# Combining one group's expert rows on chip while the other rows are read back, in a two-layer mixture-of-experts step

## The chip, the cores and the metric

One NeuronCore of a Trainium2 chip runs the whole program. The metric is the device time of one execution in microseconds (us). Three timed runs of the kernel before gave 1610.86, 1612.04 and 1613.86 us; a further execution was profiled.

## What is computed

A transformer trunk of two layers on 384 tokens of width 1024 (128 of a context pass, 256 of a denoising pass): layer 0 mixes tokens by differential attention, layer 1 by retention. Each mixer is followed by a mixture of experts, 16 experts in 4 groups of 4. All in float32.

```python
def group_moe(h, w_router, router_bias, w_gate, w_up, w_down):
    t = h.reshape(B * N, D)                       # D = 1024, 384 tokens in all
    s = sigmoid(t @ w_router)
    sel = s + router_bias
    grp_score = top_k(sel.reshape(-1, 4, 4), 2)[0].sum(-1)
    best = argmax(grp_score)                      # one group for each token
    _, idx = top_k(where(in_group, sel, -inf), 2) # two experts of that group
    gates = one_hot(idx) * normalised(s at idx)
    for each expert e:                            # w_gate, w_up: 1024 x 512, w_down: 512 x 1024
        y += (silu(t @ w_gate[e]) * (t @ w_up[e]) * gates[e]) @ w_down[e]
```

The layer then adds a per-feature gate times y to x, and a normalisation follows.

## The kernel before

**Engines.** Each engine runs its own list of instructions in order, and semaphores tie the lists together. PE (TensorE) multiplies, DVE (VectorE) and ACT (ScalarE) move and combine results, POOL (GpSimd) does some elementwise work and the indirect reads, SP issues the weight loads. `x` is kept transposed on chip as `xT`, features on partitions.

**Weights.** A ring of six slots of 2 MB holds weight units: three for each expert (gate, up, down), in the order of use. SP refills a slot when its last user is done: expert e's gate and up slots when the gate and up matmuls of expert e-2 and its overflow are done, the down slot when its down matmuls are (L530 issues).

**Routing** (`experts(l)` on DVE, L1455 to L1548). The logits and the normalisation come out of PE; DVE picks the group and the two experts of each token in some 40 small chained operations, PE computes each token's rank in its expert (L814, L816), and DVE makes the one-hot selection `sel` of pairs of experts (L1519). Meanwhile PE turns the scaled x into token rows `htok` (L807, six pieces of 128x512); ACT scales them (L1177) and POOL adds the shift (L1705).

**Experts** (PE, L880 to L915). Experts go two by two through x = 0, 1. Up to 64 tokens of an expert are gathered by one-hot matmuls from `htok` (L828) into `xs`. For expert e: gate and up (L892, L893: each 64 columns of the array), silu on ACT (L1210), the product on DVE (L1592), four transposes (L904), part of the next pair's gather, down (L913, L914), a copy by DVE (L1596), and a store of the 64 rows to the HBM table `expert_rows` by ACT (L1218). A further loop handles overflow in blocks of 32 tokens for an expert with more than 64 (L850 to L873, its rows stored by L1198). The number of blocks is read from a table at run time.

**Read-back.** When all 16 experts' rows are stored, POOL reads two rows for each token by six indirect DMAs (`pick_rows`, L1755), DVE weighs and adds them into `ytok` (L1600, L1601), PE turns `ytok` (L921, 8 jobs of three transposes), and DVE adds each times the gate to `xT` (L1363). The squares for the next norm follow on ACT (L1062).

**Order.** `plan_jobs` lists every use of a PSUM bank in PE's order, with the engine that empties it; jobs take the eight banks in turn. `plan_units` lists the weight units.

## Time and profile before

| | us |
|---|---|
| median of three runs | 1612.04 |
| profiled execution | 1609.19 |
| its span (first to last instruction) | 1607.4 |
| PE busy | 1390.9 |
| VectorE busy | 416.1 |
| ScalarE busy | 260.6 |
| GpSimd busy | 74.7 |
| data moved by DMA | 345.75 MB, mean 215 GB/s |

The span is what the trace covers; 1.8 us of the profiled execution lie around it. Busy PE means that matmuls are in flight. Layer 0's experts lie at about 386 to 703 us, layer 1's at 1233 to the end. L-numbers are lines of the kernel before.

### The profile page before, as it was taken

To read this page: it belongs to the slowest core of one execution; us is meant where nothing else is said; L and a number is where in the kernel's file an instruction comes from. 1 tells how busy PE (TensorE), PEld (TensorE's weight loads), DVE (VectorE), ACT (ScalarE), POOL (GpSimd) and SP (SyncE) were. 2 spreads that over 40 slices of the span, in tenths; PEclk is the share of its full clock that TensorE was granted. 3 is DMA by queue.
4 is the path that set the end of the run, shared out by engine and by line. 5 is a ranking of instruction groups with operands and counts; after the bars stand their busy time and mean duration, and the time that the engine had idled before them with its cause. 6 is when DMAs were issued, how large, how long until landed. Compare 5 with 4: busy or idle time off the path is not lost.

```text
span 1607.4 us, 16614 instructions
## 1 busy us (share of the span) xinstructions
PE 1390.9 (87%) x6404; PEld 729.0 (45%) x6404; DVE 416.1 (26%) x1138; ACT 260.6 (16%) x546; POOL 74.7 (5%) x97
## 2 busy tenths in 40 slices
PE   5997998698998988479999999998797898988863
PEld 3544655365443434144454544544454543443422
DVE  3234515524111111051250521603203211011113
ACT  3133114212110100021110221202102101010002
POOL 2110000001000000100000000000002000000001
PEclk9998998798999999879999999999799899999986
DMA  9888329514999998653233332333022499999403
GB/s 343 318 261 294 113 69 363 209 53 158 379 396 398 395 397 333 216 183 105 105 105 105 105 105 92 118 104 126 29 81 105 182 396 397 396 395 366 173 21 118
DMA packets 162734, 345.75 MB, mean 215 GB/s; under 512 B 5193, under 2 KB 22770, under 8 KB 162626
## 3 DMA queue, kind: packets, MB, share of 16 engines
q1 hardware_dynamic: 149906, 319.24, 54.1%
q10 hardware_dynamic: 9776, 15.34, 2.7%
q0 software_dynamic: 2944, 9.65, 2.1%
q8 instruction: 77, 1.26, 0.3%
q14 instruction: 31, 0.25, 0.0%
HBM read 324.95 MB, written 19.27 MB: 214 GB/s over the span
## 4 chain that ended last, share of the span: by engine, by line
PE 73%; DMA 11%; issue 6%; DVE 5%; ACT 3%; SPq 1%; POOL 0%; DVEq 0%; ACTq 0%; POOLq 0%
PE psum L699 18%; PE psum L892 11%; PE psum L692 10%; DMA ring<-in_moe_w_up 9%; PE psum L1007 5%; PE psum L913 5%; PE psum L828 4%; PE psum L796 3%; PE psum L992 3%; PE psum L594 2%; PE psum L861 2%; DMA ring<-in_w_ada 1%; PE psum L601 1%; PE psum L873 1%; PE psum L757 1%
## 5 line engine op out<-in xcount | busy, mean ns | idle before, releaser
L699 PE MATMUL psum<-ring,hT 128*128 128x512 f32 x672 | 289.4, 592 | 0.0
L892 PE MATMUL psum<-ring,work 128*64 128x512 f32 x512 | 234.9, 613 | 24.6 <-DMA ring<-in_moe_w_up 15.6
L893 PE MATMUL psum<-ring,work 128*64 128x512 f32 x512 | 235.3, 614 | 0.0
L699 PEld LDWEIGHTS psum<-ring,hT 128*128 128x128 f32 x672 | 127.5, 190 | 158.9 <-issue 157.8
L692 PE MATMUL psum<-hT,ring 128*128 128x384 f32 x512 | 170.9, 493 | 3.3 <-DVE hT L1348 3.3
L892 PEld LDWEIGHTS psum<-ring,work 128*64 128x64 f32 x512 | 71.2, 141 | 173.2 <-issue 172.8
L913 PE MATMUL psum<-ring,work 128*64 128x512 f32 x256 | 122.5, 623 | 11.4 <-issue 11.3
L692 PEld LDWEIGHTS psum<-hT,ring 128*128 128x128 f32 x512 | 98.6, 193 | 71.7 <-issue 6.0
L914 PE MATMUL psum<-ring,work 128*64 128x512 f32 x256 | 122.7, 624 | 0.0
L828 PE MATMUL psum<-work 128*128 128x128 f32 x768 | 107.1, 292 | 13.2 <-issue 10.9
L828 PEld LDWEIGHTS psum<-work 128*128 128x128 f32 x768 | 95.5, 200 | 37.4 <-issue 32.8
L1592 DVE TENSOR_TENSOR work<-work,psum 64x512 f32<-64x512 f32 x32 | 22.1, 690 | 242.3 <-ACT work L1210 242.3
L1596 DVE COPY work<-psum 128x512 f32<-128x512 f32 x32 | 22.1, 692 | 203.4 <-PE psum L914 203.4
L1210 ACT ACTIVATE work<-psum 64x512 f32<-64x512 f32 x32 | 18.8, 588 | 339.4 <-PE psum L893 339.4
L893 PEld LDWEIGHTS psum<-ring,work 128*64 128x64 f32 x512 | 71.1, 141 | 0.0
L913 PEld LDWEIGHTS psum<-ring,work 128*64 128x64 f32 x256 | 33.9, 143 | 73.5 <-issue 70.6
L1363 DVE SCALAR_TENSOR_TENSOR xT<-psum,mod,xT 128x128 f32<-128x128 f32 x64 | 22.5, 411 | 124.9 <-PE psum L1007 83.4
L796 PE MATMUL psum<-sq,ring 128*128 128x384 f32 x128 | 44.2, 507 | 9.0 <-DVE sq L1444 9.0
L921 PE MATMUL psum<-base_sb,sq 128*128 128x128 f32 x48 | 9.6, 390 | 46.8 <-issue 46.8
L594 PE MATMUL psum<-ring,cond 128*32 128x512 f32 x384 | 44.5, 603 | 3.7 <-DMA ring<-in_w_ada 3.7
L1007 PE MATMUL psum<-sq,ring 128*128 128x384 f32 x128 | 45.1, 507 | 0.9 <-ACT hT L1228 0.9
L1641 DVE TENSOR_SCALAR work<-psum,work 128x256 f32<-128x256 f32 x4 | 1.9, 485 | 167.1 <-PE psum L958 167.1
(287 smaller groups left out, 1394.1 us busy)
## 6 DMA issues: line engine op xcount, KB each, us to landing
ring<-in_moe_w_gate SPq DMA_DIRECT2D x32, 2048.0 KB, 17.2
ring<-in_moe_w_up SPq DMA_DIRECT2D x32, 2048.0 KB, 22.1
ring<-in_moe_w_down SPq DMA_DIRECT2D x32, 2048.0 KB, 19.2
ring<-in_w_ada SPq DMA_DIRECT2D x24, 2048.0 KB, 12.2
ring<-in_da_w_qkv SPq DMA_DIRECT2D x6, 2048.0 KB, 17.1
expert_rows<-work ACTq DMA_DIRECT2D x64, 128.0 KB, 5.6
ring<-in_ret_w_qkv SPq DMA_DIRECT2D x8, 1024.0 KB, 7.9
ring<-in_ret_w_qkv SPq DMA_DIRECT2D x4, 2048.0 KB, 8.0
```

The costliest lines, as they stand in the source:

```text
L594: last = mm(b[32 * j:32 * j + 32, :], cond[:, kt, :], w[:, kt, :], start=kt < 4, stop=kt >= 4)
L692: last = mm(b[:, 0:TOK], w[:, kt, col:col + P], hT[:, kt, :], start=kt == 0, stop=kt == KT - 1)
L699: last = mm(b, hT[:, kt, P * t:P * t + P], w[:, kt, :], start=kt == 0, stop=kt == KT - 1)
L796: last = mm(b[:, 0:TOK], w[:, h, P * (ft % 4):P * (ft % 4) + P], oT[:, h, :], start=h == 0, stop=h == HEADS - 1)
L828: last = mm(out, htok[:, t, P * kt:P * kt + P], sel[:, t].rearrange("p x s -> p (x s)"), start=t == 0, stop=t == TT - 1)
L861: last = mm(ov[OVB * j:OVB * j + OVB, 0:QC], ox[:, kt, :], w[:, kt, QC * (j % 2):QC * (j % 2) + QC], start=kt == 0, stop=kt == KT - 1)
L892: mm(psum[0:BLK, x, :], xk, wg[:, kt, :], start=kt == 0, stop=kt == KT - 1)
L893: last = mm(psum[BLK:P, x, :], xk, wu[:, kt, :], start=kt == 0, stop=kt == KT - 1)
L913: mm(psum[0:BLK, 5 + x, :], eaT[:, x, k, :], wd[:, k, 0:512], start=k == 0, stop=k == 3)
L914: last = mm(psum[BLK:P, 5 + x, :], eaT[:, x, k, :], wd[:, k, 512:D], start=k == 0, stop=k == 3)
L992: last = mm(b, a, v, start=n == 0, stop=n == len(terms) - 1)
L1007: last = mm(b[:, 0:TOK], w[:, k, P * (ft % 2):P * (ft % 2) + P], roT(k), start=k == 0, stop=k == 15)
```

## The change

The groups go in the order 3, 2, 1, 0 (router columns and bias are loaded in this order). The last group's rows (experts 12 to 15 in the new order, `LAST` = 12) are no longer stored: for each of these experts DVE makes a one-hot matrix times the gates (`selw`), PE turns it (`wT`), and matmuls of the expert's rows with `wT` give a contribution to y in feature layout, which DVE adds to `xT`. This is done while the next expert's gate and up run, two feature blocks behind every second k step; expert 15's come after its down. The rows of the first 12 experts are read back by POOL after expert 11; ACT and DVE weigh them at expert 13, and PE turns `ytok` in experts 14 and 15. Tokens of the last group read row 0 with weight zero. Gate and up of expert 2 go to two spare places outside the ring (`spare`), loaded before the experts start. The ring slots of gate and up are free when the expert's activation is transposed (`T`), not when gate and up are done. The token rows are scaled and shifted by one DVE operation, and POOL's additions go.

```diff
+GROUPS = (3, 2, 1, 0)
+LAST = NE - EPG
+def side_plan():
+    pair = lambda e, i: [("comb", e, i, 4), ("comb", e, i + 4, 7)]
+    turn = lambda i: [("turn", None, i, 2), ("turn", None, i + 1, 3)]
+    plan = {(e, 2 * i + 1): pair(e - 1, i) for e in range(LAST + 1, NE) for i in range(4)}
+    plan[(NE - 2, "T")] = turn(0)
+    for i in range(3):
+        plan[(NE - 1, 2 * i)] = turn(2 * i + 2)
...
-        out = [(("htok", layer, i), "act") for i in range(2 * TT)]
+        out = [(("htok", layer, i), "dve") for i in range(2 * TT)]
...
+        spare = [(sq, wm["yg"][:, 2 * D:3 * D]), (hT, wm["yg"][:, 0:D])]
...
+    def moe_unit(r):
+        return divmod(r if r < 6 else r + 2, 3)
...
-                for q in range(1, NE // 2):
-                    for x in range(2):
-                        e = q * 2 + x
-                        ov = sp.value_load(RT[l][0:1, e - 1:e], min_val=0, max_val=OVMAX)
-                        sp.wait_ge(m["gu"], e - 1)
-                        settle(sp, l)
-                        sp.wait_ge(m["o_down"], ov + 1)
-                        settle(sp, l)
-                        expert_load(x, 0, e)
-                        expert_load(x, 1, e)
-                        sp.wait_ge(m["down"], e - 1)
-                        settle(sp, l)
-                        expert_load(x, 2, e)
+                filled(sp, ("rwo" if l else "wo", KT - 1))
+                spare_load(0)
+                filled(sp, ("htok", l, 2 * TT - 1))
+                for i in range(2 * TT):
+                    emptied(sp, ("htok", l, i))
+                spare_load(1)
+                for r in range(6, 3 * NE - 2):
+                    e, part = moe_unit(r - 6)
+                    sp.wait_ge(m["down" if part == 2 else "T"], e + 1)
+                    settle(sp, l)
+                    expert_load(r)
...
+                def combine(e, kt, out):
+                    rows = slice(BLK * (kt // 4), BLK * (kt // 4) + BLK)
+                    return mm(out, ysb[rows, e % 2, P * (kt % 4):P * (kt % 4) + P], wT[rows, :], start=True, stop=True)
+                def side_work(at):
+                    for kind, e, kt, place, n, before_, _ in side.get(at, ()):
+                        if before_:
+                            pe.wait_ge(m["side_added"], before_)
+                        if kind == "comb":
+                            pe.wait_ge(m["y"], e + 3)
+                            pe.wait_ge(m["wT"], e - LAST + 1)
+                            last = combine(e, kt, psum[:, place, 0:TOK])
+                        else:
+                            pe.wait_ge(m["xs"], NE)
+                            pe.wait_ge(m["ytok"], TT)
+                            for t in range(TT):
+                                last = tr(psum[:, place, P * t:P * t + P], ytok[:, t, P * kt:P * kt + P], ident)
+                        last.then_inc(m["side"], 1)
...
                             last.then_inc(m["T"], 1)
+                            if e >= LAST:
+                                pe.wait_ge(m["selw"], e - LAST + 1)
...
+                                for t in range(TT):
+                                    last = tr(psum[:, 4, P * t:P * t + P], selw[:, t].rearrange("p n s -> p (n s)"), ident)
+                                last.then_inc(m["selT"], 1)
+                            side_work((e, "T"))
...
-                pe.wait_ge(m["ytok"], TT)
+                pe.wait_ge(m["y"], NE + 2)
+                pe.wait_ge(m["wT"], EPG)
+                pe.wait_ge(m["side_added"], side_count)
                 for ft in range(KT):
                     b = open_job(("y", l, ft))
-                    for t in range(TT):
-                        last = tr(b[:, P * t:P * t + P], ytok[:, t, P * ft:P * ft + P], ident)
-                    done(last)
+                    done(combine(NE - 1, ft, b[:, 0:TOK]))
...
+                            if e >= LAST:
+                                act.wait_ge(m["selT"], e - LAST + 1)
+                                A(wT, psum[:, 4, 0:TOK], ACT.Copy).then_inc(m["wT"], 1)
...
+                            if e == LAST + 1:
+                                act.wait_ge(m["picked"], 32 * TT)
+                                for t in range(TT):
+                                    A(ytok[:, t, :], yg[0][:, t, :], ACT.Copy, scale=wt_all[:, 0, t:t + 1]).then_inc(m["half"], 1)
...
+                def token_rows(half):
+                    for t in range(TT):
+                        i = TT * half + t
+                        filled(dve, ("htok", l, i))
+                        V.scalar_tensor_tensor(out=htok[:, t, 512 * half:512 * half + 512], in0=bank(("htok", l, i)), scalar=rin[:, t:t + 1],
+                                               in1=shrow[:, min(t, 1), half, :], op0=ALU.mult, op1=ALU.add).then_inc(evac["dve"], 1)
...
+                token_rows(0)
                 b3 = rbias[:, :].unsqueeze(1).broadcast_to([P, TT, NE])
...
                 dve.wait_ge(m["chosen"], 1)
...
+                token_rows(1)
...
+                def side_work(at):
+                    for kind, e, kt, place, n, _, added in side.get(at, ()):
+                        if added:
+                            dve.wait_ge(m["side_added"], added)
+                        dve.wait_ge(m["side"], n + 1)
+                        add_rows(psum[:, place, :], kt).then_inc(m["side_added"], 1)
...
+                            if e >= LAST:
+                                weigh_slots(e)
+                            for kt in range(KT):
+                                side_work((e, kt))
...
+                            if e == LAST + 1:
+                                for t in range(TT):
+                                    dve.wait_ge(m["half"], t + 1)
+                                    V.scalar_tensor_tensor(out=ytok[:, t, :], in0=yg[1][:, t, :], scalar=wt[:, 1, t:t + 1], in1=ytok[:, t, :],
+                                                           op0=ALU.mult, op1=ALU.add).then_inc(m["ytok"], 1)
...
+            for g in range(NG):
+                here, there = slice(EPG * g, EPG * g + EPG), slice(EPG * GROUPS[g], EPG * GROUPS[g] + EPG)
+                pool.dma_start(rbias[:, here], ins["router_bias"].unsqueeze(0)[:, there].broadcast_to([P, EPG])).then_inc(in_bc, 16)
+                pool.dma_start(wr[:, :, here], ins["w_router"].rearrange("(k p) e -> p k e", p=P)[:, :, there]).then_inc(in_bc, 16)
...
-                pool.wait_ge(m["stored0"], 32 * (NE // 2 + 1))
+                pool.wait_ge(m["stored0"], 32 * (LAST // 2 + 1))
...
-            add_shift(1)
+            pool.wait_ge(M[1]["routed"], 1)
             for kt in range(KT):
                 G.tensor_scalar(gdiag[:, kt, :], ident, cols1[:, kt:kt + 1], None, ALU.mult).then_inc(gdiag_ready, 1)
```

Overflow blocks of the last group (experts 12 to 15) would be combined in the same way; those of the others are stored as before.

## Rows read from the trace of the kernel before

**Rows 1.** The page's chain of work that ended last, by line.
```profile
PE psum L699 18%; PE psum L892 11%; PE psum L692 10%; DMA ring<-in_moe_w_up 9%; PE psum L1007 5%; PE psum L913 5%; PE psum L828 4%; PE psum L796 3%; PE psum L992 3%; PE psum L594 2%; PE psum L861 2%; DMA ring<-in_w_ada 1%; PE psum L601 1%; PE psum L873 1%; PE psum L757 1%
```

**Rows 2.** Windows: stretch, its length, busy time by engine, granted clock, DMA share, GB/s.
```profile
410.00:600.00 190.00, 173.95 (x908) 81.63 (x906) 21.91 (x42) 18.83 (x36) 0.00 (x0) 0.96 1.04 397
...
666.00:690.00 24.00, 0.61 (x5) 0.53 (x4) 6.63 (x7) 0.00 (x0) 5.78 (x6) 0.61 0.66 219
1563.00:1587.00 24.00, 0.61 (x4) 0.39 (x3) 6.63 (x7) 0.00 (x0) 5.74 (x6) 0.56 0.44 142
```

**Rows 3.** Timeline (start, length, both us) behind layer 0's last expert, all engines.
```profile
666.15 0.69 DVE L1596 COPY work<-psum 128x512 f32<-128x512 f32 x1 [4.79 <-PE psum L914]
666.87 1.13 ACTq L1218 DMA_DIRECT2D expert_rows<-work  x2
670.87 1.05 POOL L1755 DMA_INDIRECT work<-expert_rows,work  x1 [291.05 <-issue]
...
677.23 0.94 POOL L1755 DMA_INDIRECT hT<-expert_rows,work  x1 [0.30 <-issue]
...
683.36 0.75 DVE L1600 TENSOR_SCALAR sq<-work 128x1024 f32<-128x1024 f32 x1 [16.52 <-DMA hT<-expert_rows,work]
...
689.50 0.87 PE L921 MATMUL psum<-base_sb,sq 128*128 128x128 f32 x3 [23.39 <-issue]
```

**Rows 4.** Timeline behind layer 1's last expert, PE's restart.
```profile
1586.64 0.66 PE L921 MATMUL psum<-base_sb,sq 128*128 128x128 f32 x2 [23.39 <-issue]
```

**Rows 5.** Timeline of PE: first gate matmuls of experts 0, 2, 3, 6, 12, 13, 14; 0, 13, 14.
```profile
394.17 0.64 PE L892 MATMUL psum<-ring,work 128*64 128x512 f32 x1
...
423.10 0.59 PE L892 MATMUL psum<-ring,work 128*64 128x512 f32 x1
...
437.01 0.59 PE L892 MATMUL psum<-ring,work 128*64 128x512 f32 x1
...
484.35 0.61 PE L892 MATMUL psum<-ring,work 128*64 128x512 f32 x1 [1.37 <-issue]
...
586.60 0.59 PE L892 MATMUL psum<-ring,work 128*64 128x512 f32 x1
...
601.60 0.61 PE L892 MATMUL psum<-ring,work 128*64 128x512 f32 x1 [0.92 <-DMA ring<-in_moe_w_up]
...
626.80 0.59 PE L892 MATMUL psum<-ring,work 128*64 128x512 f32 x1
...
1258.09 0.64 PE L892 MATMUL psum<-ring,work 128*64 128x512 f32 x1
...
1475.46 0.59 PE L892 MATMUL psum<-ring,work 128*64 128x512 f32 x1
...
1511.30 0.59 PE L892 MATMUL psum<-ring,work 128*64 128x512 f32 x1
```

**Rows 6.** The page's DMA issues: count, KB each, median us to landing.
```profile
ring<-in_moe_w_up SPq DMA_DIRECT2D x32, 2048.0 KB, 22.1
```

**Rows 7.** Timeline of PE in layer 0, of VectorE in layer 1.
```profile
369.72 2.82 PE L807 MATMUL psum<-base_sb,hT 128*128 128x128 f32 x24
...
1228.73 0.74 DVE L1363 SCALAR_TENSOR_TENSOR xT<-psum,mod,xT 128x128 f32<-128x128 f32 x2 [8.99 <-PE psum L1007]
```

**Rows 8.** Timeline of GpSimd and VectorE, at the start and in layer 0's routing.
```profile
44.06 0.72 POOL L1735 TENSOR_TENSOR work<-work 128x256 f32<-128x256 f32 x1 [6.55 <-ACT work L1100]
...
372.38 7.43 POOL L1705 TENSOR_TENSOR work<-work 128x512 f32<-128x512 f32 x6 [154.65 <-ACT work L1177]
...
373.73 1.21 DVE L1485 TENSOR_TENSOR work<-work,base_sb 128x12 f32<-128x12 f32 x1
...
380.40 0.21 DVE L1485 TENSOR_TENSOR work<-work,base_sb 128x48 f32<-128x48 f32 x1
```

**Rows 9.** The chain of work in order of time: start, us, what.
```profile
182.63 5.16 PE psum L692 x16
```

**Rows 10.** Groups of instructions: busy us, mean ns, idle before.
```profile
L1554 DVE SCALAR_TENSOR_TENSOR work<-work,base_sb 128x96 f32<-128x96 f32 x39 | 10.0, 256 | 1.3 <-issue 0.4
```

More of the change, by code:

```diff
@@ L179, in plan_units @@
     units += [(("ada", l, u), ("ada", l, u)) for l, u in NORM_UNITS]
-    units += [(("moe", 0, n), None) for n in range(3 * NE)]
+    units += [(("moe", 0, n), None) for n in range(3 * NE - 2)]
     for h in range(RH):
@@ L184, in plan_units @@
     units += [(("rwo", n), ("rwo", 2 * n + 1)) for n in range(4)]
-    units += [(("moe", 1, n), None) for n in range(3 * NE)]
+    units += [(("moe", 1, n), None) for n in range(3 * NE - 2)]
     return units
@@ L820, in experts @@
                 u0 = unit_no[("moe", l, 0)]
-                emptied(pe, ("rank", l))
+                for i in range(2 * TT):
+                    emptied(pe, ("htok", l, i))
                 def gather(half, kts):
@@ L1759, in _ @@
             pool.sem_inc(M[1]["o_down"], 1)
-            add_shift(0)
             pick_rows(0)
```

259 lines of the change are left out of this document (171 added, 88 removed).

## The prediction

> **What bounds the kernel now.** I read the chain that ended last, by line, first: TensorE's matmuls hold most of it, and one transfer stands out, the experts' up weights with 9% [rows 1]. Then the stages: through 190 us of the first layer's experts the DMA engines move 397 GB/s at a busy share of 1.04 while PE is busy 174 us; in the 24 us after the last expert of either layer PE works 0.6 us and the transfers run at 219 and 142 GB/s [rows 2]. So there are two bounds: weight traffic while experts run, and a latency chain behind them. The timeline shows that chain: the last copy of expert rows at 666.15, the store issued at 666.87, six indirect reads from 670.87 to 678.2 whose last lands at 683.3 (what VectorE's wait ends on), six weighting operations, and PE's transposes at 689.50 after 23.39 us of idleness; layer 1 has the same 23.39 [rows 3, 4]. Last, the starts of the experts on PE. Undisturbed an expert takes 437.01 - 423.10 = 13.9 us. Where weights bound it, six take 586.60 - 484.35 = 102.3, so 17.0 each, with some restarts of PE in it. One expert moves 3 x 2.097 MB plus 0.26 MB of stored rows, 6.55 MB, at 397 GB/s 16.5 us [rows 2, 5, 6]; I use 16.7. An expert with one overflow block takes 626.80 - 601.60 = 25.2, one with two 1511.30 - 1475.46 = 35.8 [rows 5]: 11.3 and 22 more. The trace has two blocks in layer 0 (experts 13, 14) and five in layer 1 (12 to 15, expert 13 twice): all in the group that now comes first.
>
> **The sum's base.** The profiled execution took 1609.2 us (span 1607.4 and 1.8 around it), 2.8 below the median 1612.0. I sum against 1609.2 and add 2.8 at the end.
>
> **Head of the experts.** The token rows' scaling leaves ScalarE, the shift leaves GpSimd, both become one VectorE operation per piece. No row has it; a 128x128 and a 128x256 one with a PSUM input take 0.74 us together [rows 7], so 0.7 to 0.8 for 512 columns. Six cost 4.4 us in VectorE's chain, of which the last three replace a wait for the rank matmuls (about 2 us), so 1.5 + 0.7 are on the path. Removed is what GpSimd did to that chain: an operation on 12 columns takes 1.21 us while GpSimd's 7.43 us run, and on 48 columns 0.21 after it [rows 8]. Six operations are stretched so, to 0.8 to 1.2 each, about 5.4 us together. Net 3.1 us earlier in layer 0, 4.2 in layer 1 (four NORM additions fewer on the path, and GpSimd's eight diagonal products leave it too). Bounds 0 to 5 each. The moved diagonal products now run beside VectorE's index computation, 5 to 10 us long, which has the 8 us of the first gather and 7 us of the first gate and up as cover. The "GPSIMD Engine Reference" of the Trainium skill (its table's row on SBUF interfaces) says that GpSimd's SBUF interfaces are shared with VectorE. By it the index chain stretches as these rows did; the cover still holds it. The six more small loads on GpSimd's queue near the start, at 0.94 to 1.05 each as its other DMAs [rows 3], stay under the 6.55 us in which it idles there [rows 8]: nothing, else under 1 us.
>
> **Early overflow and the two spare weight slots.** Experts start at 391.1 instead of 394.17 [rows 5]. Expert 0 takes 13.9, experts 1 and 2 take 25.2, then 13.9 each: expert 4 starts at 469.3, expert 7 could at 511. A slot is now refilled after the activation's transpose, 9.6 us after an expert's start (7.0 gate and up, 2.3 gather, 0.4), so behind an overflow. The DMA queue runs dry three times while experts 1 and 2 are long, about 25 us in all; the two spare slots let PE not feel it. It is full from expert 3's transpose (465.0): the first load lands 9 us later (5.3 to move; the rest is an estimate from the reads' 6.1 between issue and landing [rows 3]) and each next one 5.57 (16.7 / 3), so expert 6's up weights land at 496.6, expert 7's at 513.3: from here the weights bound, 16.7 each. Expert 12 starts at 596.9 and 13 could at 613.6. In layer 1 the start is 1253.9, expert 0 takes 25.2, 1 takes 36, 2 and 3 take 25.2, expert 7 starts at 1409.1, 12 at 1492.6. The DMA queue is never dry after that: at a transpose some four units are queued ahead.
>
> **The read-back moves into this stretch.** Expert 11 ends at 594. Between its last store and the first read lay 4.0 us in a half idle queue [rows 3]; I take twice that in a full one. Six indirect reads from 602.5, 1.25 to 1.3 apart as in the tail, are issued by 610 [rows 3]. Their 3.1 MB take 7.9 us of the DMA engines at 397 GB/s. Expert 13's weights are late by all of it or, where reads share the queue with loads already due, by 5: it starts at 618.6 to 621.5. That gives 5 to 8 us per layer of the tail back. What weighs the rows has slack: PE needs them after expert 14's transposes, at about 652, ScalarE's wait for them is reached at about 634, and they are there by about 622. The "DMA: Bandwidth & Descriptors" page of the Trainium skill (Queues, rings and completion order) says that a DMA engine takes its queues in turn, packet by packet. By it the reads get half the engines beside the full load queue, 16 us, and land at 622 as said; no row shows two full queues.
>
> **Added work in the last group.** A combining matmul has 64 partitions and 384 columns; the nearest rows, 16 records for 8 matmuls of 384 columns in 5.16 us, give 0.645 each [rows 9]; below, half of that, if two run at a time. Eight per expert for 13, 14 and 15: 5.2 us (2.6 to 5.2; I take 5.2). Turning the weighted one-hot rows: three transposes, 24 take 2.82 us at full clock [rows 7], so 0.35. The turns of ytok, 24, 2.8, moved off the tail. On VectorE each of these feeds an add of 0.74 (0.82 if the two halves don't overlap) [rows 7], plus seven small operations per expert near the 0.26 us row [rows 10], 1.8.
> Expert 12: 14.3. Expert 13: 13.9 + 5.2 + 0.35, 19.6. Expert 14, bound by VectorE: copy 0.75, the three ytok operations 3.9 (three pairs took 6.14, the other half 0.75 each [rows 3]), 1.8, eight adds 6.6, gating 0.7, then transposes, down and its waits 5.5: 19.3. Expert 15: 7.0 + 5.2 + 2.1 on PE against 14.1 on VectorE, then gating and the rest, 19.8. Nothing hides these except the weights' own pace: expert 14's are there at 637, so it is PE and VectorE that bound the last three.
> Last down in layer 0: 618.6 or 621.5 + 19.6 + 19.3 + 19.8 = 677.3 to 680.2. Layer 1: 1572.6 to 1575.5.
>
> **The tail.** Store, reads, weighting and 23.39 us of idleness go; what is left is the copy (0.69) and a semaphore, 0.9. PE restarts at 678.2 to 681.1 instead of 689.50, and at 1573.5 to 1576.4 instead of 1586.64 [rows 3, 4]: 8.4 to 11.3 and 10.2 to 13.1 gained. The eight last combinations, 5.2 us, replace 24 transposes that took 5.4 after the idleness. I take 10 and 11.5. The granted clock was 0.61 and 0.56 in the idle stretches [rows 2] and should stay higher now, worth 1 to 2 us after each; I set that against as much lost where PE changes between halves and whole arrays. The "TensorEngine Tiling (Array Packing)" page of the Trainium skill (Key Properties) says that a change of tiling mode drains TensorE, which speaks against this change: 24 changes per layer. By it a few us more would be lost; no row of mine separates it.
> 1609.2 - 10 - 11.5 = 1587.7, plus 2.8: **1590.5 us**.
>
> **Rivals.**
> (a) *The pairs of combinations run side by side* on the two halves of the array, and the reads cost only what they overlap: expert 13 falls by 2.6, expert 15's PE part drops below VectorE's, the reads cost 5. 4 to 5 per layer: 1582. For it: an expert's 24 matmuls of 512 columns at the price of rows 9 would be 20.6 us, more than its whole 13.9 [rows 5], so pairs on column halves do overlap. Against: VectorE still bounds 14 and 15. The same skill page (Tiling Modes) has two 64x128 tiles, and would give this.
> (b) *The read-back is not hidden*: stores, six reads and the full load queue take over 30 us instead of 22, ScalarE sits in its wait with expert 14's activation behind it, and PE behind that. For it: full engines from 596 on. Against: 12 us of slack. Some 5 to 8 us late per layer: 1604.
> (c) *Slower: VectorE's adds bound the last two experts.* Each add waits for its matmul, its predecessor and a bank, and PE waits for the add before it reuses bank 4 or 7. With 22 adds in experts 14 and 15, 10.8 us per layer are gone when an add costs 0.5 us more than 0.8: from 1.3 us on the change is slower. At 1.7 it is 1590.5 + 2 x 22 x 0.9 = 1630; at 1.5, 1621. For it: every add is in lockstep with PE. Against: 0.74 measured, and in the old tail eight came 0.66 apart.
> (d) *The change only moves the time*: the dry queue costs more than I find, because PE catches up with the weights already at expert 5, and with 8 us of reads the end of the experts moves 10 us more per layer: 1610.
>
> **Chances.** Forecast 0.62, (a) 0.14, (b) 0.10, (c) 0.07, (d) 0.07. Its own range is 1585 to 1598. The range that takes in (a) and most of (b), and the bounds of head and combinations, is 1576 to 1606. A difference under 0.2%, 3 us, can't be told from none. Faster: the forecast, (a), (b) and a little of (d), 0.87; same 0.05; slower 0.08.
>
> **What would show it.** Right: PE idle under 1.5 us after the last down; gather about 3 to 4 us earlier; small VectorE operations there at 0.2; DMA below 300 GB/s while experts 0 to 3 run and 397 after 4; expert 13 with the longest wait for weights; last three experts 19 to 20 each. Wrong: ScalarE waiting for the reads (b), adds above 1.3 us apart (c), the weights' wait beginning at expert 5 (d), combinations 0.32 apart (a). The whole is wrong if the last expert ends later than 689 or 1586.

## The result and the profile after

The changed kernel took 1617.4 us (median of 20 runs, 1607.5 to 1620.2), the kernel before 1610.3 (20 runs, 1602.8 to 1616.8): a ratio of 1.0031, 95% interval 1.0017 to 1.0046. I had forecast 1590.5 with a range that ended at 1606. The change costs about 5 us by this ratio (7 by the medians) where I expected 21 to be gained.

The profiled execution of the changed kernel took 1607.5 us (span 1605.6), the shortest of its twenty, so its total may not be laid beside the 1609.2 of before. Its stages may. From the first turn of the token rows to the first product of the next stage, layer 0 took 707.05 - 362.28 = 344.8 us against 702.94 - 369.72 = 333.2 before: 11.6 longer. Layer 1, to the end, took 1605.65 - 1236.45 = 369.2 against 373.8: 4.6 shorter. Together 7.0 slower, near what the medians say. What this execution has less lies elsewhere: 7.4 us ahead of layer 0's experts, in code that the change hardly touches, and 1.2 between the two layers. The output product of the first mixer started at 308.12; in a second profile of the same kernel at 319.92, in the one before at 315.59, and in all fifteen profiles of this study between 308 and 321. In the second profile the two stages of experts, each as a whole, have the same length to 0.3 us.

Head and tail went as forecast. PE's rows of the head, layer 0 and layer 1 (the token rows' first turn, the gather, expert 0):
```profile
362.28 0.52 PE L844 MATMUL psum<-base_sb,hT 128*128 128x128 f32 x3
...
374.55 8.54 PE L866 MATMUL psum<-work 128*128 128x128 f32 x48 [2.44 <-DVE work L1634]
...
383.02 0.64 PE L980 MATMUL psum<-ring,work 128*64 128x512 f32 x1
...
1236.45 0.41 PE L844 MATMUL psum<-base_sb,work 128*128 128x128 f32 x2
...
1255.07 0.64 PE L980 MATMUL psum<-ring,work 128*64 128x512 f32 x1
```
Expert 0 starts 20.7 and 18.6 us after the first turn, where it was 24.45 and 24.55: 3.7 and 5.9 gained (forecast 3.1 and 4.2). VectorE's operation on 48 columns at the gather takes 0.20 and none of the small ones is stretched to the 1.2 us of [rows 8].

The tail of both layers, all engines:
```profile
692.79 0.69 DVE L1769 COPY work<-psum 128x512 f32<-128x512 f32 x1 [6.48 <-PE psum L1012]
...
693.54 4.24 PE L947 MATMUL psum<-work 64*128 64x384 f32 x16 [0.79 <-DVE work L1769]
...
694.55 5.29 DVE L1468 SCALAR_TENSOR_TENSOR xT<-psum,mod,xT 128x128 f32<-128x128 f32 x16 [1.07 <-PE psum L947]
...
1584.90 4.24 PE L947 MATMUL psum<-work 64*128 64x384 f32 x16 [0.79 <-DVE work L1769]
```
PE restarts 0.75 us after the copy begins; it was 23.35 [rows 3, 4]. From the last down product to the next stage 14.3 and 21.6 us are left of 36.9 and 44.1.

So the loss is among the experts: from expert 0 to the last down product 309.7 us instead of 271.9 in layer 0, 329.0 instead of 305.1 in layer 1. Windows (columns as in [rows 2]): experts 4 to 11, then experts 13 to 15 of layer 0 and of layer 1.
```profile
466.00:595.00 129.00, 116.46 (x612) 54.48 (x608) 15.40 (x29) 12.55 (x24) 0.00 (x0) 0.97 1.04 396
```
```profile
618.92:692.72 73.80, 62.50 (x261) 24.01 (x261) 32.83 (x86) 8.09 (x13) 0.00 (x0) 0.86 0.67 245
1516.18:1584.08 67.90, 60.05 (x261) 21.87 (x261) 32.74 (x86) 8.09 (x13) 0.00 (x0) 0.89 0.56 214
```
The three experts that I had put at 58.7 us take 73.8 and 67.9. VectorE is busy 33 us of them and the DMA engines 0.67 and 0.56 of the time. PE is busy 60 to 62.5 us, at a mean granted clock of 0.86 to 0.89 (0.97 in the experts before). So nothing but PE is near full, and PE is often at its lower clock level. That is how it would look if PE and VectorE waited for each other; the experiments test it. PE's first gate products of experts 12, 13, 14 and 15:
```profile
595.20 0.61 PE L980 MATMUL psum<-ring,work 128*64 128x512 f32 x1 [0.65 <-issue]
...
618.92 1.09 PE L980 MATMUL psum<-ring,work 128*64 128x512 f32 x1 [8.12 <-DMA ring<-in_moe_w_up]
...
645.61 0.59 PE L980 MATMUL psum<-ring,work 128*64 128x512 f32 x1
...
670.36 0.59 PE L980 MATMUL psum<-ring,work 128*64 128x512 f32 x1
```
Expert 13 waits 8.12 us for its weights, then takes 26.7; expert 14 takes 24.8, expert 15 22.4. Layer 1 has 21.0, 26.2 and 20.7. I had put 19.6, 19.3 and 19.8, so the excess is 7.1, 5.4 and 2.6 in layer 0 and 1.4, 6.9 and 0.9 in layer 1.

The 7.1 of expert 13 in layer 0 are mostly something else. Between the first and the second of the transposes of its activation PE stands still, and the profile shows nothing that it waits for ("issue"):
```profile
638.22 0.48 PE L994 MATMUL psum<-base_sb,work 64*128 64x64 f32 x3 [3.35 <-issue]
```
From these transposes to the down product it takes 6.15 us instead of 1.54 in layer 1, and the down product, partly at the lower clock level, 5.03 instead of 3.65: 6.0 us together. The trace has a DMA queue that it calls "instruction", with loads of 16 KB. One starts at 635.68, inside the stop, and PE goes on 2.54 us later. Ten profiles of the changed kernel and its variants have a stop at this very transpose, of 0.6 to 3.4 us, and in all ten PE goes on 2.3 to 2.6 us after such a load's start. So PE probably waits there for instructions; no run varies this alone.

Expert 14 of layer 1 shows how the waits arise (all engines, from the copy of expert 13's rows to the transposes):
```profile
1537.39 0.69 DVE L1769 COPY work<-psum 128x512 f32<-128x512 f32 x1 [5.92 <-PE psum L1012]
...
1538.11 3.68 DVE L1773 SCALAR_TENSOR_TENSOR sq<-hT,work,sq 128x1024 f32<-128x1024 f32 x3
...
1538.99 0.92 PE L947 MATMUL psum<-work 64*128 64x384 f32 x4
...
1541.71 0.25 DVE L1679 SCALAR_TENSOR_TENSOR work<-work,base_sb 128x96 f32<-128x96 f32 x1
1541.88 0.85 DVE L1684 TENSOR_SCALAR work<-base_sb,work 128x128 f32<-128x128 f32 x3
1542.65 0.85 DVE L1690 TENSOR_SCALAR work<-base_sb,work 128x128 f32<-128x128 f32 x3
1543.41 1.39 DVE L1696 SCALAR_TENSOR_TENSOR xT<-psum,mod,xT 128x128 f32<-128x128 f32 x4
...
1544.21 2.29 PE L947 MATMUL psum<-work 64*128 64x384 f32 x4 [2.44 <-DVE xT L1696]
...
1546.43 1.11 PE L980 MATMUL psum<-ring,work 128*64 128x512 f32 x1
...
1554.48 1.39 DVE L1696 SCALAR_TENSOR_TENSOR xT<-psum,mod,xT 128x128 f32<-128x128 f32 x4 [1.32 <-PE psum L947]
1555.90 0.69 DVE L1763 TENSOR_TENSOR work<-work,psum 64x512 f32<-64x512 f32 x1
...
1556.74 0.43 PE L994 MATMUL psum<-base_sb,work 64*128 64x64 f32 x4 [2.36 <-DVE work L1763]
```
PE's first pair of combinations of expert 13's rows (four records, two products) runs at 1538.99 and takes 0.92 us. Its adds could follow at once, but VectorE is in ytok's 3.68 us and then in the next slots' 1.95; they begin 3.5 us after the pair's end. PE stands 2.44 us before the next pair, and when it goes on its products of 512 columns take 1.11 us instead of 0.59: it has fallen to the 1.2 GHz level. At the end the gating stands behind the last two adds, and the transposes wait 2.36 us.

### The profile page after: what moved, and what is told of

The parts are those of the page before. It is cut to its first block, busy times and chain, and to the rows that moved or that the text cites. A ratio compares the mean times of both kernels' runs of the same rounds, so it can differ in the third digit from the quotient of the medians.

```text
span 1605.6 us, 17122 instructions
## 1 busy us (share of the span) xinstructions
PE 1425.1 (89%) x6556; PEld 731.6 (46%) x6556; DVE 466.5 (29%) x1332; ACT 263.9 (16%) x548; POOL 64.3 (4%) x91
## 4 chain that ended last, share of the span: by engine, by line
PE 75%; DMA 11%; DVE 6%; ACT 3%; issue 3%; SPq 1%; DVEq 0%; POOL 0%; ACTq 0%; POOLq 0%
PE psum L736 18%; PE psum L980 11%; PE psum L729 10%; DMA ring<-in_moe_w_up 9%; PE psum L1104 5%; PE psum L866 5%; PE psum L1011 5%; PE psum L833 3%; PE psum L1089 3%; PE psum L947 2%; PE psum L918 2%; PE psum L631 2%; DMA ring<-in_da_w_qkv 1%; PE psum L930 1%; PE psum L794 1%
## 5 line engine op out<-in xcount | busy, mean ns | idle before, releaser
L980 PE MATMUL psum<-ring,work 128*64 128x512 f32 x480 | 228.8, 623 | 33.0 <-DMA ring<-in_moe_w_up 21.8
L981 PE MATMUL psum<-ring,work 128*64 128x512 f32 x480 | 229.2, 624 | 0.0
L980 PEld LDWEIGHTS psum<-ring,work 128*64 128x64 f32 x480 | 64.9, 142 | 173.4 <-issue 173.2
L1011 PE MATMUL psum<-ring,work 128*64 128x512 f32 x256 | 121.9, 621 | 0.7 <-issue 0.5
L1012 PE MATMUL psum<-ring,work 128*64 128x512 f32 x256 | 122.0, 621 | 0.0
L981 PEld LDWEIGHTS psum<-ring,work 128*64 128x64 f32 x480 | 64.9, 142 | 0.0
L1011 PEld LDWEIGHTS psum<-ring,work 128*64 128x64 f32 x256 | 33.7, 142 | 63.2 <-issue 60.1
L1696 DVE SCALAR_TENSOR_TENSOR xT<-psum,mod,xT 128x128 f32<-128x128 f32 (+1 forms) x128 | 44.6, 410 | 50.2 <-PE psum L947 46.2
L1468 DVE SCALAR_TENSOR_TENSOR xT<-psum,mod,xT 128x128 f32<-128x128 f32 x64 | 22.5, 411 | 124.8 <-PE psum L1104 83.3
```

The costliest lines, as they stand in the source:

```text
L980: mm(psum[0:BLK, x, :], xk, wg[kt], start=kt == 0, stop=kt == KT - 1)
L981: last = mm(psum[BLK:P, x, :], xk, wu[kt], start=kt == 0, stop=kt == KT - 1)
L1011: mm(psum[0:BLK, 5 + x, :], eaT[:, x, k, :], wd[k][:, 0:512], start=k == 0, stop=k == 3)
L1012: last = mm(psum[BLK:P, 5 + x, :], eaT[:, x, k, :], wd[k][:, 512:D], start=k == 0, stop=k == 3)
L1696: last = V.scalar_tensor_tensor(out=xT[:, kt, a:z], in0=src[:, a:z], scalar=mod[:, l, 40 + kt, c:c + 1], in1=xT[:, kt, a:z], op0=ALU.mult, ...
```

## Experiments

All ratios are to the kernel before, which ran on the same chip beside each; "n us below the changed kernel" is the difference of two such ratios, with 1.0031 and 1.0015 for the changed kernel, times 1610; "last three" is from expert 13's first gate product to the last down product, layer 0 / layer 1, read from each run's trace.

**The same kernel again.**


> The changed kernel once more, unaltered. Its profiled execution so far took 1607.5 us, its median 1617.4, while the kernel before had 1609.2 and 1610.3. Theory 1 (the extra 10 us of a usual execution lie in the last group of four experts, where PE alternates with VectorE and falls to the lower clock level): this profile reads 1613 to 1619, the last three experts take 75 to 80 us in layer 0 and 69 to 75 in layer 1 (73.8 and 67.9 in the first profile), the attention part up to the output product stays near 308. Rival (the first profile only had a lucky attention part): the output product starts at 313 to 317 instead of 308.1, and the expert stages keep 309.7 and 329.0 within 2 us.


1615.3 us median of 12, ratio 1.0015 (0.9996 to 1.0034), the profiled execution 1619.2. Of the rival, the experts' half held: the stages agree to 0.3 us (309.6, 328.9; last three 74.1 / 68.0). The output product started late, at 319.92, even later than the 313 to 317 that it named.
```profile
319.92 1.65 PE L833 MATMUL psum<-sq,ring 128*128 128x384 f32 x2 [8.96 <-DVE sq L1549]
```
Theory 1 was wrong: the last three did not grow (it wanted 75 to 80 and 69 to 75), and the first mixer did. For all that follows I compare stages, not totals of single profiles.

**The order alone**, in the kernel before:
```
+GROUPS = (3, 2, 1, 0)
-w = (wg, wu, wd)[part][e].rearrange(...)
+w = (wg, wu, wd)[part][EPG * GROUPS[e // EPG] + e % EPG].rearrange(...)
```


> The kernel before with its groups in the order 3 to 0 and nothing else. Theory 1 (the order is neutral: the DMA queue is dry early instead of late): the stage from expert 0 to the last down product takes 268 to 276 us in layer 0 (271.9 before) and 298 to 306 in layer 1 (305.1), total within 5 us of the kernel before. Rival (the early overflow starves the queue and PE never gets it back): 280 or more in layer 0 and 313 or more in layer 1, total 1620 to 1630.


1610.1, ratio 0.9984 (0.9962 to 1.0005). Experts 272.1 and 306.1 us (271.9 and 305.1 before). Theory 1: overflow blocks cost the same at either end, so rival (d) of the prediction falls as far as it rests on the order. This trace shows one thing more: with the old ring of six slots expert 12 starts 206.6 and 239.3 us after expert 0, in layer 0 sooner than in any profile of the changed kernel (210.7 and 212.2), in layer 1 the same. Expert 0 took 14.6 us there in layer 0 and not 16.7 to 18.4. The two spare places and the later return of the slots bought nothing that these traces show.

**The head alone**, in the kernel before (token rows on VectorE, GpSimd's addition out, and as in the changed kernel seven small VectorE operations that normalise the routing weights moved behind the slot table, 1.5 us):
```
-A(htok[...], bank(("htok", l, i)), ACT.Copy, scale=rin[:, t:t + 1])
-G.tensor_tensor(cols, cols, shrow[:, min(t, 1), half, :], ALU.add)
+V.scalar_tensor_tensor(out=htok[...], in0=bank(("htok", l, i)), scalar=rin[...], in1=shrow[...], ...)
```


> The kernel before with the head's part alone: token rows scaled and shifted by VectorE in one operation, no GpSimd addition, the normalisation of the routing weights behind the slot table. Theory 1 (the head's gain is real and is kept by the weight-bound stage, because slots are refilled earlier too): expert 0 starts 3 to 4 us after the rows' first turn earlier than before in layer 0 (20.7 instead of 24.45) and 4 to 6 earlier in layer 1, total 1601 to 1605. Rival (weights bound the end of the stage anyway, the gain turns into a longer wait for weights): same starts, but the stages from expert 0 to the last down product are 3 to 5 us longer, total 1608 to 1612.


1598.8, ratio 0.9921 (0.9893 to 0.9950). Expert 0 starts 20.7 and 18.7 us after the first turn. In its one profile layer 0's experts took 276.0 us, 4.1 longer, of which experts 13 and 15 have 1.7 each, at granted clocks of 0.94 and 0.89 where it was 1.00, and layer 1's 305.5; the medians say that the gain is kept: 0.5 to 1.1%, 8 to 17 us. The head alone was worth more than half of what I had forecast for the whole change, and the rest of the change lost it all again and 5 us more.

**The changed kernel with the order 0 to 3.**
```
-GROUPS = (3, 2, 1, 0)
+GROUPS = (0, 1, 2, 3)
```


> The changed kernel with its groups in the order 0 to 3, so that the group with most overflow blocks is the one combined on chip. Theory 1 (order is neutral for the weights; the read-back of 3.1 MB, which delays expert 13 by 8 us when weights bound it, is hidden behind the overflow blocks of experts 13 and 14, but each block's own eight combinations and adds cost 6 us): expert 13 waits under 2 us for weights, two blocks in layer 0 and five in layer 1 add 12 and 30 us; total 1615 to 1635. Rival (order 3 to 0 is what loses, by the queue that is dry for 25 us): total 1600 or less.


1669.4, ratio 1.0366 (1.0335 to 1.0397). Worse than either theory. Experts 13 to 15, layer 0 and 1:
```profile
604.14:712.32 108.18, 82.92 (x547) 34.62 (x547) 49.79 (x138) 9.82 (x17) 0.00 (x0) 0.87 0.45 165
1496.71:1644.53 147.82, 105.46 (x835) 45.05 (x831) 69.34 (x198) 11.55 (x21) 0.00 (x0) 0.86 0.21 79
```
Expert 13, with one block in layer 0, took 43.1 us where it had taken 26.7 without one; expert 14 44.4 instead of 24.8. So a block whose rows are combined on chip costs 16 to 20 us, not 11.3. In layer 0 the read-back was not hidden either: expert 13 waited 6.7 us. In layer 1, behind the block of expert 12, it did not wait. The order is free in itself, but with on-chip combination it must be 3 to 0: for the data of this run that is worth 52 to 56 us.

**Without the side products.**
```
-plan = {(e, 2 * i + 1): pair(e - 1, i) for e in range(LAST + 1, NE) for i in range(4)}
+plan = {}
```


> The changed kernel without the 24 combining products of experts 12 to 14 and their adds on VectorE (this part of the sum is left out; the weighted rows, their turns, the read-back and expert 15's products stay). Theory 1 (the last group was mis-sized because the side products hold PE in lockstep with VectorE): from expert 13's start to the last down product 48 to 53 us in each layer instead of 73.8 to 76.1 and 68, the half clock stretches in expert 14 disappear, total 40 us below the changed kernel. Rival (ytok, the weighted rows and their turns are what holds it): 62 or more in either layer.


1583.7, ratio 0.9815 (0.9761 to 0.9868).
```profile
629.62:682.31 52.69, 45.88 (x213) 19.00 (x213) 16.21 (x38) 8.10 (x13) 0.00 (x0) 0.91 0.91 337
1511.18:1562.26 51.08, 44.94 (x213) 19.39 (x213) 16.12 (x38) 8.10 (x13) 0.00 (x0) 0.91 0.70 265
```
52.7 / 51.1, theory 1 in the stages, though the total is 32 to 35 us below the changed kernel and not 40: the 24 products and their adds cost 21 us in layer 0 and 17 in layer 1. Without them expert 13 of layer 0 has no stop at its transposes, so some 6 of the 21 may be that stop and the clock behind it. I had given the whole added work of the three experts 58.7 - 3 x 13.9 = 17 us, ytok and slots included.

**The products without VectorE's adds.**
```
-add_rows(psum[:, place, :], kt).then_inc(m["side_added"], 1)
+dve.sem_inc(m["side_added"], 1)
```


> The changed kernel with all its side products on TensorE but without VectorE's 32 adds of them per layer (the residual stream misses these rows); VectorE only passes the semaphore on. Theory 1 (VectorE's adds, not TensorE's products, are the price): the last three experts take 55 to 60 us, 10 to 18 less than in the changed kernel in each layer. Rival (the products and the changes between half and whole arrays cost as much by themselves): 65 or more.


1594.7, ratio 0.9879 (0.9824 to 0.9935).
```profile
627.88:690.23 62.35, 57.38 (x261) 22.00 (x261) 10.63 (x22) 8.09 (x13) 0.00 (x0) 0.91 0.79 290
1514.86:1571.50 56.64, 54.38 (x261) 20.55 (x261) 10.64 (x22) 8.09 (x13) 0.00 (x0) 0.96 0.67 254
```
62.4 / 56.6, a little over the forecast in layer 0. Taking out the adds saves 11.5 and 11.3 us. That is of all 32 adds, the eight behind the turns of ytok too, so the 24 have at most this share of the 21 and 17, and the products (with the stop in layer 0, which stays) at least the other 9.7 and 5.6. VectorE's busy time fell by 22 us, twice what the stretch lost: half of the adds' time had been hidden. Expert 14 without adds needs 10.0 us for gate and up with three pairs of products among them, 3.0 over the plain 7.0: 0.5 per product.

**Without the read-back.**
```
-pool.indirect_dma_start(out=yg[c][:, t, :], ...).then_inc(m["picked"], 16)   (six of them)
```


> The changed kernel without the six indirect reads (the rows of the first three groups are not read back). Theory 1 (they cost the weight stream exactly their own bytes): expert 13's wait for its weights shrinks from 8.1 to 9.3 us (7 to 8 in layer 1) to 1 to 3 us, as of the experts before it; the last three experts stay at 74 to 76 and 68; total 14 us below the changed kernel. Rival (the wait is that of the queue behind the early overflow): it stays above 5 us.


1598.1, ratio 0.9919 (0.9891 to 0.9947), theory 1. Expert 13's wait shrinks from 8.12 to 0.92 us (in layer 1 from 7.81 to 2.09):
```profile
617.73 0.61 PE L980 MATMUL psum<-ring,work 128*64 128x512 f32 x1 [0.92 <-DMA ring<-in_moe_w_up]
```
Expert 12 takes 16.5 us to the next start instead of 21.1 to 24.9; the last three 72.0 / 65.8, 2 us less: expert 13's first products now run at 0.61 us and its gate and up take 10.1 us instead of 12.1, PE no longer having stood still before them. So the read-back delays expert 13 by 4.6 to 8.4 us per layer, as forecast (5 to 8).

**ytok weighed earlier.** ScalarE's three scalings ahead of expert 13's activation, VectorE's three operations behind expert 13's gating:
```
-if e == LAST + 1: (after the copy of y)
+if e == LAST + 1: (after side_work((e, "T")), before dve.wait_ge(m["down"], e + 1))
     V.scalar_tensor_tensor(out=ytok[:, t, :], in0=yg[1][:, t, :], ...)
```


> The changed kernel with ScalarE's three scalings ahead of expert 13's activation and VectorE's three weighting operations behind expert 13's gating instead of ahead of expert 14's adds. Theory 1 (in expert 14 TensorE stands behind 3.7 us of weighting and 2 us of small operations in VectorE, loses about 5 us to it and 3 more to the lower clock level): expert 14's gate and up stretch falls from 14.8 to 16.4 us to 12 to 13, the three weighting operations vanish between expert 13's transposes and its down product, total 5 to 8 us below the changed kernel. Rival (VectorE is the bound of the whole stretch, so the 3.7 us only move into expert 13): under 2 us.


1605.0, ratio 0.9965 (0.9940 to 0.9989), 8 to 11 us below the changed kernel by the two ratios of that one; its experts' stages are 10.8 us shorter, more than expected. Last three 68.4 / 62.6. VectorE in layer 1, in expert 13 (the weighting) and 14 (two pairs of adds):
```profile
1529.39 3.68 DVE L1769 SCALAR_TENSOR_TENSOR sq<-hT,work,sq 128x1024 f32<-128x1024 f32 x3
...
1537.89 1.39 DVE L1696 SCALAR_TENSOR_TENSOR xT<-psum,mod,xT 128x128 f32<-128x128 f32 x4
1540.61 1.39 DVE L1696 SCALAR_TENSOR_TENSOR xT<-psum,mod,xT 128x128 f32<-128x128 f32 x4 [1.32 <-PE psum L947]
```
Gate and up take 10.0 us, as without any add: once VectorE arrives in time, its adds (1.39 of every 2.72 us) hide behind PE completely. 3.7 us of work in the wrong place cost 5.4 us of the last three in layer 0 and 5.3 in layer 1.

**Gating ahead of the last adds.**
```
-for kt in range(KT):
+for kt in range(KT - 1):
     side_work((e, kt))
 V.tensor_tensor(ea[...], sg[...], psum[...], ALU.mult).then_inc(m["gated"], 1)
+side_work((e, KT - 1))
```
and PE turns the weighted slots last before the down product.


> The changed kernel with VectorE's gating of experts 13 to 15 ahead of the last pair of adds instead of behind it, and the turn of the weighted one-hot rows issued last before the down product. Theory 1 (gating stands 1.4 us behind the two last adds, which nothing on TensorE needs that early): from the end of gate and up to the transposes 1.2 us less in each of the three experts (3.65 becomes 2.4 in expert 15), 3.5 per layer, total 6 to 8 us below the changed kernel. Rival (TensorE waits for the same adds anyway, before it reuses bank 4): under 2 us.


1608.6, ratio 0.9991 (0.9971 to 1.0011), 4 to 6 below the changed kernel, between the two theories; last three 68.3 / 64.0. The transposes' wait falls to 0.71 us (2.36 before), but the next turn then waits for the same adds:
```profile
1578.40 0.43 PE L994 MATMUL psum<-base_sb,work 64*128 64x64 f32 x4 [0.71 <-DVE work L1763]
...
1579.77 0.52 PE L1005 MATMUL psum<-base_sb,work 128*128 128x128 f32 x3 [0.94 <-DVE xT L1696]
```
Expert 15's down starts 0.8 us earlier, not 1.2; the larger part came from expert 14, 3.2 and 3.1 us shorter, where the down product also ran at the full clock (3.65 us, 4.2 and 5.35 before). A part of this gain is the clock's.

**Combinations in the wait for weights.**
```
+plan[(LAST + 1, -1)] = [job for i in range(4) for job in plan.pop((LAST + 1, 2 * i + 1))]
+side_work((e, -1))
 wg, wu = unit(e, 0), unit(e, 1)
```


> The changed kernel with expert 12's eight combinations ahead of expert 13's first weight instead of between its gate and up products. Theory 1 (TensorE stands idle there for 8 us, because the read-back takes them from the weight stream; the combinations with their adds, some 8 us in lockstep, fit into it): expert 13's gate and up stretch falls from 12.1 to 12.4 us to 7.0 to 8.8, its start moves by less than 1 us, total 7 to 9 us below the changed kernel. Rival (VectorE is busy with expert 13's slots and the lockstep takes over 10 us, so expert 13 starts later by what it saves): under 2 us.


1602.0, ratio 0.9951 (0.9928 to 0.9973), 10 to 13 us below the changed kernel. Last three 60.0 / 59.3, expert 13's start 1.1 and 1.3 us later. Its gate and up take 7.1 and 8.5 us instead of 12.1 and 12.3; in layer 0 its stop of 3.35 us and its down product at the lower clock level are gone too, so the stages are 18 us shorter, twice what I expected.

**All three.**


> The changed kernel with all three: ytok weighed in expert 13, gating ahead of the last adds, expert 12's combinations in the wait for expert 13's weights. If the three gains add up (11 us of the first, 6 to 8, 7 to 9), the last three experts take 59 to 62 us per layer and the median is 1587 to 1594, 1.1 to 1.5% below the kernel before. If VectorE's total work bounds the stretch instead, they overlap: 64 us or more per layer and 1598 or more.


1589.9, ratio 0.9855 (0.9830 to 0.9880). Windows of experts 13 to 15, and PE's timeline while the weights of expert 13 come in:
```profile
627.68:685.43 57.75, 52.02 (x245) 19.91 (x245) 29.61 (x80) 8.11 (x13) 0.00 (x0) 0.96 0.83 308
1510.23:1566.65 56.42, 51.98 (x246) 19.53 (x245) 29.60 (x79) 8.11 (x13) 0.00 (x0) 0.94 0.66 249
```
```profile
1502.10 0.98 PE L949 MATMUL psum<-work 64*128 64x384 f32 x4 [0.79 <-DVE work L1779]
...
1505.66 4.63 PE L949 MATMUL psum<-work 64*128 64x384 f32 x8 [0.18 <-DVE xT L1699]
...
1510.23 1.11 PE L983 MATMUL psum<-ring,work 128*64 128x512 f32 x1
```
The expectation for gains that add up held. VectorE is busy 29.6 us of it, and does nearly all of its adds for expert 12 ahead of it; the stretch is 16.1 and 11.5 us shorter than in the changed kernel, the clock 0.96 and 0.94. Since expert 12's products now stand ahead of the stretch, the whole stages say it better: 292.8 and 318.9 us, 16.9 and 10.1 shorter. In layer 0 some 5 of this are the stop at expert 13's transposes (0.66 us now) and the clock behind it. Not one operation was taken out: this part of the loss was one of order, not of work. Beside the head alone, 0.9921, the ratio 0.9855 also says what combining on chip is worth once it is well placed: some 10 us.

**An earlier return of the weight slots**, in the changed kernel and in the combined one:
```
+gather(x, range(4 * x, 4 * x + 3), m["freed"])      (its first product signals)
-sp.wait_ge(m["down" if part == 2 else "T"], e + 1)
+sp.wait_ge(m["down" if part == 2 else "freed" if e < NE - 2 else "T"], e + 1)
```


> The changed kernel with a gate or up slot given back at the first gathering product behind the expert's gate and up (and its overflow) instead of at its transposes, 2.6 us later. Theory 1 (the weight stream is unbroken from expert 3's slot on, so whatever delays that point, its 2.7 us half clock and issue stall too, delays expert 12 by as much: 210.0 to 212.2 us after expert 0 in layer 0, where I had forecast 205.8): expert 12 starts 2 to 3 us sooner after expert 0 in both layers, total 4 to 6 us below the changed kernel. Rival (the stream is bound by its own bytes from the first load, 397 GB/s, and the early stalls are not passed on): expert 12 starts within 1 us of where it did.


1611.8, ratio 0.9999 (0.9985 to 1.0013), 3 to 5 us below the changed kernel, which is little beside the intervals. Expert 12 starts 207.4 and 237.4 us after expert 0 (212.2 and 238.9; in the second profile 210.7 and 239.8). What decides is read from expert 3's transposes to expert 12's start, in the changed kernel, layer 0 and 1:
```profile
461.58 0.46 PE L994 MATMUL psum<-base_sb,work 64*128 64x64 f32 x4
...
595.20 0.61 PE L980 MATMUL psum<-ring,work 128*64 128x512 f32 x1 [0.65 <-issue]
...
1360.70 0.46 PE L994 MATMUL psum<-base_sb,work 64*128 64x64 f32 x4
...
1493.95 0.61 PE L980 MATMUL psum<-ring,work 128*64 128x512 f32 x1 [1.11 <-issue]
```
133.6 and 133.3 us; in the nine executions of this study with the order 3 to 0, the spare slots and the late return, 18 stretches, it is 133.2 to 134.2. Here it is
```profile
474.22 0.46 PE L997 MATMUL psum<-base_sb,work 64*128 64x64 f32 x4
...
603.05 0.61 PE L983 MATMUL psum<-ring,work 128*64 128x512 f32 x1 [2.49 <-issue]
```
128.8, and 131.4 in layer 1. The return itself shows it better. In the eighteen stretches SyncE issues the gate load for that slot 0.6 to 0.8 us behind the transposes, and expert 12 starts 132.7 to 133.4 us after this issue. Here the issue comes 4.0 and 1.6 us ahead of the transposes (in layer 0 a stop of PE, 2.22 us, lies between), and expert 12 starts 132.8 and 133.0 us after it. With both changes together, the next run, it is 135.3 and 133.1; for the 135.3 I have no reason. So the stream is unbroken from that issue on in all but this stretch, and what is late ahead of it is late at expert 12.


> The combined version with the same earlier return of the slots. Theory 1: 2 to 3 us less per layer between expert 0 and expert 12, the last three experts unchanged at 56 to 58 us, median 1583 to 1587. Rival (the weights' gain turns into idle time elsewhere, the last group being bound by TensorE and VectorE): 1588 to 1592, as the combined version.


1583.9, ratio 0.9825 (0.9801 to 0.9849), the fastest kernel of this study that computes everything: 26.8 us below the kernel before in their medians. Last three 55.1 / 53.8, where I had expected them unchanged. In its profile expert 12 started 2.1 and 1.5 us sooner, but expert 13's wait grew (expert 12 took 29.3 and 24.6 to the next start), so the gain over the combined version lies in the last three; whether the return of the slots caused that, or ordinary variation, one profile each can't tell.

## Why the prediction was wrong, point by point

*The head* (-3.1, -4.2): right in place, somewhat small: -3.7 and -5.9. GpSimd's additions did stretch VectorE's small operations: the six from 372.89 to 379.88 in the trace before take 6.62 us together and 1.10 in the changed kernel (a reduction among them 0.17 in both). That agrees with the Trainium skill, "GPSIMD Engine Reference", on the shared SBUF interfaces.

*The early overflow* (expert 12 205.8 us after expert 0 in layer 0, 238.7 in layer 1): 210.2 to 212.8 in layer 0, 238.8 to 241.1 in layer 1, without the earlier return. The mechanism and the 16.7 us per expert were right: from expert 3's transposes I had 596.9 - 465.0 = 131.9 and found 133.2 to 134.2. What I missed is that expert 3 reaches them late. I let expert 0 take 13.9 us; in the two profiles it took 18.4 and 16.7, with a stop of PE that the profile calls issue, and in expert 3 stood another, of 2.36 and 2.23 us. In both profiles an instruction load, as in expert 13, starts within 0.2 us of the beginning of either stop. The first, in expert 0:
```profile
393.02 1.86 PE L866 MATMUL psum<-work 128*128 128x128 f32 x13 [2.90 <-issue]
```
The trace of before has such stops and longer experts 0 and 3 too, 15.0 and 18.0 us, but there weights bound the following experts and swallow them. Here they lie ahead of the point from which the queue is full. Some 5 us in layer 0, half of the 10 that rival (d) named, and next to nothing in layer 1.

*The read-back* (expert 13 delayed by 5 to 8 us): right. Expert 12 took 23.7 and 22.2 us to the next start (24.9 and 21.1 in the second profile), and 16.5 in both without reads. ScalarE never held PE up over them, so rival (b) did not come in. "DMA: Bandwidth & Descriptors" of the Trainium skill (Queues, rings and completion order) has each engine take its queues in turn, packet by packet. The trace agrees: from 607 to 619 us, beside a full load queue, the reads moved 740 packets and the weights 744. The last read landed at 622.75, the 622 that I had worked out.

*The added work of the last group* (19.6 + 19.3 + 19.8 = 58.7): **this step failed**, 73.8 to 74.1 in layer 0 and 68 in layer 1, so 24 to 25 of the 28 us that the stages miss the forecast's -21.5 by. The wrong part is the overlap: I let VectorE's and PE's work in these experts hide behind each other. The operations themselves cost about what I took for them: the adds of one pair 1.39 us (0.70 each, I took 0.74 to 0.82), ytok 3.68 (3.9), the small ones 1.95 (1.8), a product 0.5 (0.645; rival (a) had 0.32). For expert 14 I summed VectorE's work and let PE's hide behind it. But the two take turns: PE, in its program order, may not pass a combination whose bank has not been added yet, so its gate and up products don't run while it waits for VectorE, and VectorE has nothing to add while PE is back at them. Time then goes by the sum of the waits, not by the fuller engine. ytok and the slots ahead of the first add cost the first turn, gating behind the last adds the last one, and each stop let the clock fall. The combined kernel only reorders, makes the three experts 16.1 and 11.5 us shorter (some 4 of them because expert 12's products run in the wait), and then takes 57.7 and 56.4. That this lies near my 58.7 is partly luck, since expert 12's products no longer stand in it. About 6 of layer 0's 15 us are not this: they are the stop of 3.35 us in expert 13, its return to work and the clock behind it, which both profiles of the changed kernel have and which I had nowhere. Without them layer 0 misses by 9, as layer 1 does.

*Rival (c)*, slower by VectorE's adds, was the one on the right side, and it named the mechanism: every add in lockstep with PE. Its sign came too, adds over 1.3 us apart: the eight of expert 14 in layer 1 lie between 1543.41 and 1555.87, 1.56 each, and at 1.5 it gave 1621. But I asked how dear an add is (0.70 us), and put 0.07 on it for that. The distance is no sign by itself: in the kernel with ytok early it is 1.36 and VectorE's adds are hidden. What counted was the adds' place in VectorE's order.

*The change of tiling modes*: I had set a few us against a gain in clock. The Trainium skill's "TensorEngine Tiling (Array Packing)" says that a mode switch drains TensorE. With adds on time, a pair of products with its two switches takes 2.72 - 4 x 0.43 = 1.0 us of PE, less than the 1.29 that I had put down for the two products alone; what a drain costs is in that 1.0, and no run here separates it. The clock did not rise; it was 0.86 to 0.89 in the last three instead of 0.97 and 0.96 before (there with overflow blocks among them).

*The tail*: PE's idleness shrinks from 23.4 to 0.8 us, as forecast, and the way to the next stage by 22.5 us in either layer.

*The sum's base*: laying one execution's total beside another's would have misled here by 7 to 9 us; the stages did not. Two of my sums are off by less than half a microsecond (expert 13 adds up to 19.45, layer 1's last down product to 1573.0 at the earliest), which changes nothing.

## What to carry to other kernels

Work slipped between the products of a busy engine can be priced by the handshakes and not by its busy time: for each bank that two engines share, write down who stands ahead of the other engine's operation in its queue, and put nothing long there (a weighting, the next slots), nor such an operation ahead of one that the first engine waits for (the last adds ahead of the gating). Put such work first where the engine waits anyway, here for weights. Where a transfer stream becomes unbroken at one event, every delay ahead of that event counts in full, even one that was free in the kernel before.

## What the runs showed of the hardware that I had not expected

- Two products on 64 partitions each, in the two halves of the array, overlap in part: a pair takes 0.92 us and eight in a row 4.24, 0.53 each, where one of 384 columns on the whole array takes 0.645 [rows 9]; the granted clock was 1.00 in both stretches.
- Gaps of PE over 0.9 us that are marked issue stand in all fifteen profiles (10 to 17 each, the two tails of the old kind among them), many at the gather's products of the same experts. A part of them, those of experts 0 and 3 and of expert 13 in layer 0 among them, begin within 1 us of a 16 KB load of the queue called instruction. Most such loads, about two in each expert, come without a stop. No experiment here varies them.
- The first mixer's length varies from run to run with unchanged code: the stretch from its first value projection to its second query projection took 81.3 to 88.2 us.
- Behind the 8.12 us without products PE worked at the 1.2 GHz level: expert 13's first products took 1.06 to 1.09 us, at 2.4 GHz 0.59; behind a wait of 0.92 us, without the reads, 0.61.
